# Norm tiles made in step with the output projection at two borders, and weight loads moved between state stores

## The reference, cut to what matters

```python
def rmsnorm(x, g):
    y = xf * lax.rsqrt(jnp.mean(xf * xf, axis=-1, keepdims=True) + EPS)
    return y * g
def ffn_half(x, g, wg, wu, wd):
    return x + 0.5 * swiglu(rmsnorm(x, g), wg, wu, wd)
# layer i:
xp = ffn_half(xp, *f1);  xp = xp + mixer(rmsnorm(xp, norm_mix[i]));  xp = ffn_half(xp, *f2)
```

## Time and profile before

| | us |
|---|---|
| median of 3 runs (1693.33 to 1696.01) | 1695.6 |
| the profiled execution, its time | 1693.2 |
| its span | 1691.4 |
| PE busy in it | 1655.1 (98%) |
| DVE, ACT, POOL busy | 823.6, 633.9, 283.7 |
| granted clock of PE, mean | 0.996 of full |

### The profile page before, as it was taken

One profiled execution on the slowest core, in us unless ns is written; L12 is line 12 of the kernel. 1 busy time (PEld: TensorE's weight loads), 2 busy tenths in 40 slices (PEclk: granted clock), 3 DMA queues, 4 the chain that ended last, 5 costly groups with the idle time before them and its releaser, 6 DMA issues.

```text
span 1691.4 us, 25177 instructions
## 1 busy us (share of the span) xinstructions
PE 1655.1 (98%) x9539; PEld 1581.4 (93%) x9539; DVE 823.6 (49%) x969; ACT 633.9 (37%) x765; POOL 283.7 (17%) x253
## 2 busy tenths in 40 slices
PE   7999999999999999999999999999999999999997
PEld 6999999976799999999999999898989888999997
DVE  6444444753355444445444444564646466444332
ACT  5343322354334433224344322333333344444232
POOL 2111122430031111121111022202020212111021
PEclk9999999999999999999999999999999999999999
DMA  5444344540024444345444344647475754444342
GB/s 164 124 124 128 113 120 135 164 152 32 32 75 125 126 129 123 106 128 141 129 130 128 95 125 132 239 161 257 166 253 171 251 182 124 124 124 124 103 120 89
DMA packets 341736, 231.25 MB, mean 137 GB/s; under 512 B 8429, under 2 KB 312634, under 8 KB 341690
## 3 DMA queue, kind: packets, MB, share of 16 engines
q1 hardware_dynamic: 341690, 230.61, 45.5%
HBM read 209.64 MB, written 20.94 MB: 136 GB/s over the span
## 4 chain that ended last, share of the span: by engine, by line
PE 94%; DVE 3%; ACT 1%; DMA 1%; issue 1%; SPq 0%; POOL 0%; DVEq 0%; POOLq 0%; ACTq 0%
PE bank L140 27%; PE bank L142 27%; PE bank L141 26%; PE bank L820 2%; PE bank L1332 1%; PE bank L1334 1%; PE bank L1333 1%; PE bank L841 1%; PE bank L1369 1%; PE bank L1399 1%; DMA RAW<-w_ffn_up_dram 1%; DVE WL L134 1%; PE bank L1440 1%; DVE XL L152 0%; PE bank L1358 0%
## 5 line engine op out<-in xcount | busy, mean ns | idle before, releaser
L140 PE MATMUL bank<-XH,WH 128*128 128x384 f32 x1776 | 600.1, 338 | 5.8 <-DVE XL L152 5.7
L142 PE MATMUL bank<-XH,WL 128*128 128x384 f32 x1776 | 595.3, 335 | 0.0
L141 PE MATMUL bank<-XL,WH 128*128 128x384 f32 x1776 | 595.1, 335 | 0.0
L127 ACT ACTIVATE WH<-RAW 128x2048 fp32r<-128x2048 f32 (+2 forms) x199 | 337.0, 1695 | 622.6 <-PE bank L142 578.8
L134 DVE TENSOR_TENSOR WL<-RAW,WH 128x2048 fp32r<-128x2048 f32 (+2 forms) x199 | 408.2, 2053 | 298.8 <-ACT WH L127 298.5
L140 PEld LDWEIGHTS bank<-XH,WH 128*128 128x128 f32 x1776 | 334.7, 188 | 13.8 <-issue 7.4
L141 PEld LDWEIGHTS bank<-XL,WH 128*128 128x128 f32 x1776 | 335.0, 189 | 1.1
L142 PEld LDWEIGHTS bank<-XH,WL 128*128 128x128 f32 x1776 | 334.8, 188 | 0.0
L140 PE MATMUL bank<-AH,WH 128*128 128x384 f32 x704 | 238.3, 339 | 0.0
L141 PE MATMUL bank<-AL,WH 128*128 128x384 f32 x704 | 237.8, 338 | 0.0
L142 PE MATMUL bank<-AH,WL 128*128 128x384 f32 x704 | 237.8, 338 | 0.0
(11 more groups left out here) (224 smaller groups left out, 1463.5 us busy)
## 6 DMA issues: line engine op xcount, KB each, us to landing
RAW<-w_ffn_gate_dram SPq DMA_DIRECT2D x88, 512.0 KB, 4.0
RAW<-w_ffn_up_dram SPq DMA_DIRECT2D x88, 512.0 KB, 5.2
RAW<-w_ffn_down_dram SPq DMA_DIRECT2D x64, 384.0 KB, 4.0
RAW<-w_ret_in_dram SPq DMA_DIRECT2D x48, 512.0 KB, 4.7
RAW<-w_ffn_down_dram SPq DMA_DIRECT2D x64, 320.0 KB, 3.3
st<-state_ret_dram SPq DMA_DIRECT2D x32, 512.0 KB, 7.2
new_state_sample_dram<-st SPq DMA_DIRECT2D x32, 512.0 KB, 6.2
RAW<-w_ret_out_dram SPq DMA_DIRECT2D x16, 512.0 KB, 4.2
```

Source lines behind the costliest of these rows:

```text
L127: ins = act.activation(dst(WH), src, ACT.Copy)
L140: pe.matmul(ps, wh, xh, start=first, stop=False)
L141: pe.matmul(ps, wh, xl, start=False, stop=False)
L142: return pe.matmul(ps, wl, xh, start=False, stop=last)
```

## The change

It has four parts.

1. Behind MLA the norm tiles go to tiles of their own, `X2H` and `X2L`, which the next FFN reads. ACT makes two of them behind each of its looks, DVE one behind each add into `X` (one tile late).
2. Behind retention DVE makes tile m-1 behind the add of tile m in the last head. ACT's order is as before.
3. In both FFNs that follow, PE waits at the start for the banks instead of relying on the norm tiles for it: for 7 adds behind MLA, and for the seventh add of the last head behind retention (32 counts, one of them POOL's).
4. SP loads the last FFN's chunk 0 ahead of the last head's first group of state stores, and its chunk 1 between the first and the second group.

```diff
-        def norm_tile_act(act, s, m, g, base=0):
+        def norm_tile_act(act, s, m, g, base=0, xh=XH):
...
-        def norm_tile_dve(dve, s, m, g):
+        def norm_tile_dve(dve, s, m, g, xh=XH, xl=XL):
             dve.wait_ge(sem("xh"), m + (KD * s + 1))
...
+                if self.banks_free:
+                    pe.wait_ge(sem(f"x_ready{self.s}"), self.banks_free)
                 gate_pair(0, True)
...
@@ Mla.act
-                for q in range(7, 6 + KD // 2):
-                    self.look_act(act, q)
                 act.wait_ge(sem("stored"), 16 * 2 * TT)
-                act.wait_ge(multiplied, self.c0 + self.N_CHUNKS)
-                for m in range(KD):
-                    norm_tile_act(act, self.s + 1, m, gain(KD * (self.s + 1) + m))
-                self.look_act(act, 6 + KD // 2)
+                for g in range(KD // 2):
+                    self.look_act(act, 7 + g)
+                    for m in (2 * g, 2 * g + 1):
+                        norm_tile_act(act, self.s + 1, m, gain(KD * (self.s + 1) + m), xh=X2H)
@@ Mla.dve
-                    if g < KD // 2 - 1:
-                        self.look_dve(dve, 7 + g)
-                dve.wait_ge(sem("stored"), 16 * 2 * TT)
-                for m in range(KD):
-                    norm_tile_dve(dve, self.s + 1, m, gain(KD * (self.s + 1) + m))
-                self.look_dve(dve, 6 + KD // 2)
+                        if part:
+                            self.look_dve(dve, 7 + g)
+                        if g == 0 and part == 0:
+                            dve.wait_ge(sem("stored"), 16 * 2 * TT)
+                        if m >= 1:
+                            norm_tile_dve(dve, self.s + 1, m - 1, gain(KD * (self.s + 1) + m - 1), X2H, X2L)
+                norm_tile_dve(dve, self.s + 1, KD - 1, gain(KD * (self.s + 2) - 1), X2H, X2L)
@@ Retention.sp
-                for group in range(3):
-                    store_states(RET_HEADS - 1, group)
+                self.next_ffn.load_gate(sp, 0, 0)
+                store_states(RET_HEADS - 1, 0)
+                self.next_ffn.load_gate(sp, 0, 1)
+                store_states(RET_HEADS - 1, 1)
+                store_states(RET_HEADS - 1, 2)
@@ Retention.dve
-                self.dve_head(dve, RET_HEADS - 1)
-                for m in range(KD):
-                    norm_tile_dve(dve, self.s + 1, m, gain(KD * (self.s + 1) + m))
+                self.dve_head(dve, RET_HEADS - 1, True)
+                norm_tile_dve(dve, self.s + 1, KD - 1, gain(KD * (self.s + 2) - 1))
                 self.look_dve(dve, RET_HEADS - 1, self.PER - 1)
@@ Retention.dve_head
+                    if last and m >= 1:
+                        norm_tile_dve(dve, self.s + 1, m - 1, gain(KD * (self.s + 1) + m - 1))
@@ phases
-                  Ffn(2, 1, 1, 3, c_mla + Mla.N_CHUNKS + C, whole), Retention(4, c_ret), Ffn(3, 1, 2, 5, c_last, half)]
+        last_ffn = Ffn(3, 1, 2, 5, c_last, half, banks_free=KD * RET_HEADS)
+                  Ffn(2, 1, 1, 3, c_mla + Mla.N_CHUNKS + C, whole), Retention(4, c_ret, last_ffn), last_ffn]
```

More of the change, by code:

```diff
@@ L93, in stream_kernel @@
             ytok = sb("ytok", [P, TT, D_MODEL], F32, r)
+            X2H = sb("X2H", [P, KD, T], F32R, r)
+            X2L = sb("X2L", [P, KD, T], F32R, r)
         with ExitStack() as r:
@@ L142, in product @@
             return pe.matmul(ps, wl, xh, start=False, stop=last)
-        def norm_tile_act(act, s, m, g, base=0):
+        def norm_tile_act(act, s, m, g, base=0, xh=XH):
             act.wait_ge(sem(f"x_ready{s}"), m + (base + 1))
-            act.activation(tile(XH, m), tile(X, m), ACT.Copy, scale=g).then_inc(sem("xh"), 1)
-        def norm_tile_dve(dve, s, m, g):
+            act.activation(tile(xh, m), tile(X, m), ACT.Copy, scale=g).then_inc(sem("xh"), 1)
+        def norm_tile_dve(dve, s, m, g, xh=XH, xl=XL):
             dve.wait_ge(sem("xh"), m + (KD * s + 1))
-            dve.scalar_tensor_tensor(tile(XL, m), tile(X, m), g, tile(XH, m).bitcast(F32),
+            dve.scalar_tensor_tensor(tile(xl, m), tile(X, m), g, tile(xh, m).bitcast(F32),
                                      ALU.mult, ALU.subtract).then_inc(sem("xl"), 1)
@@ L263, in stream_kernel, with __init__ @@
         class Ffn:
-            def __init__(self, f, li, which, s, c0, next_widths):
+            def __init__(self, f, li, which, s, c0, next_widths, xh=XH, xl=XL, banks_free=0):
+                self.xh, self.xl, self.banks_free = xh, xl, banks_free
                 self.f, self.s, self.c0, self.c1 = f, s, c0, c0 + KF
@@ L285, in sp @@
             def sp(self, sp):
-                first = 1 if self.c0 == 0 else 0
+                first = 1 if self.c0 == 0 or self.last else 0
                 with sp.Fori(first, KF // 2) as i:
@@ L314, in gate_pair @@
                                     pe.wait_ge(sem("xl"), KD * self.s + k + 1)
-                                mm = product(pe, ps[:, 0:T], w, k, XH[:, k, :], XL[:, k, :], k == 0, k == KD - 1)
+                                mm = product(pe, ps[:, 0:T], w, k, self.xh[:, k, :], self.xl[:, k, :], k == 0, k == KD - 1)
                             mm.then_inc(multiplied if part else self.gate_done, 1)
@@ L1194, in stream_kernel, with __init__ @@
             PARTS = 6
-            def __init__(self, s, c0):
-                self.s, self.c0 = s, c0
+            def __init__(self, s, c0, next_ffn):
+                self.s, self.c0, self.next_ffn = s, c0, next_ffn
                 self.stored = (sem("r_stored0"), sem("r_stored1"), sem("r_stored2"))
@@ L1542, in dve, with dve_head @@
                 norm_root_dve(dve, self.s + 1)
-            def dve_head(self, dve, h):
+            def dve_head(self, dve, h, last=False):
                 c = self.c0 + self.PER * h
@@ L1666, in stream_kernel @@
         whole, half = (SLOT, SLOT), (0, 0)
-        phases = [Ffn(0, 0, 1, 0, 0, whole), Mla(1, c_mla, whole), Ffn(1, 0, 2, 2, c_mla + Mla.N_CHUNKS, whole),
-                  Ffn(2, 1, 1, 3, c_mla + Mla.N_CHUNKS + C, whole), Retention(4, c_ret), Ffn(3, 1, 2, 5, c_last, half)]
+        last_ffn = Ffn(3, 1, 2, 5, c_last, half, banks_free=KD * RET_HEADS)
+        phases = [Ffn(0, 0, 1, 0, 0, whole), Mla(1, c_mla, whole), Ffn(1, 0, 2, 2, c_mla + Mla.N_CHUNKS, whole, X2H, X2L, KD - 1),
+                  Ffn(2, 1, 1, 3, c_mla + Mla.N_CHUNKS + C, whole), Retention(4, c_ret, last_ffn), last_ffn]
         block = ctx.enter_context(nc.Block())
```

## The result

The changed kernel takes 1702.9 us (median of 5 runs, 1699.87 to 1704.14), the kernel before 1695.83 (median of 5). The ratio is 1.0042, with a 95% interval of 1.0031 to 1.0053: **7.1 us slower**, outside my range (1694.0 to 1700.5), on the side that I had given a chance of 0.27. The profiled execution took 1702.9 us with a span of 1701.1, 9.7 more than the one of before.

The account below looks back on a forecast made before the run. PE was taken as the bound, busy 98% of the span, so only border waits or clock could change. Terms -0.55 + 1.2 + 2.4 = +3.05 us on the median 1695.6 gave 1698.6 us, range 1694.0 to 1700.5.

Parts of the forecast that it names:

- MLA's tiles, own operands: MLA border: tiles 0 to 5 made during the projection, while DVE and ACT sit idle, at no cost.
- rival D: MLA border: the clock falls there too, behind the new 2.4 us stand; up to 3.4 us more loss; chance 0.12.
- The MLA border, -0.55: Sum of acc 0.55 us earlier, with tiles 6 and 7 late behind chunk 1's split; bounds nothing to 3.1.
- Loads between stores: Retention border: ACT's 12.92 us wait for chunk 0 goes, PE's matmul replaces it; ACT's split ends 4.2 us earlier.
- Retention's tiles in step, +1.2: Retention border: POOL takes turns with DVE, PE waits 5.7 us for acc, the sum comes 1.2 us later.
- The clock behind that wait, +2.4: Last FFN: PE's 5.7 us wait for acc takes the clock down to 1.2 GHz, losing 2.4 us.
- rival B: Retention border: clock falls in the first stand, the wait for acc is 2.5 us; +0.65 to +1.7 us; chance 0.26.
- A: Retention border: first stand of 3.2 us leaves the clock, the second takes it down; +2 to +4.3 us; chance 0.42.
- The sum: Whole kernel: -0.55 + 1.2 + 2.4 = +3.05 us, put on the median of 1695.6.

Follow-up runs that it names:

- e1: The changed kernel with 128 bytes of padding ahead of X2H, nothing else: 1700.12 us against 1695.42 for the kernel before.
- e2: The changed kernel with the retention border's edits taken back, so only the MLA part: 1698.5 us against 1695.42 for the kernel before.
- e3: The changed kernel with the MLA border's edits taken back, so only the retention part: 1697.69 us against 1695.42 for the kernel before.
- e6: The kernel before with AH 32 and AL 256 bytes past a multiple of 512: 1689.89 us (one run) against 1694.52.
- e10: The kernel before with 384 bytes of padding ahead of all tiles: 1692.61 us (one run) against 1695.26.
- e4: The kernel before with only SP's load order at the retention border changed (chunk loads between stores): 1692.99 us against 1695.42.
- e5: The kernel before with 128 bytes of padding ahead of AH, which shifts AH and AL: 1687.06 us against 1694.52.
- e8: e3 with DVE's split of chunk 1 held back until POOL has made all of acc: 1695.43 us against 1694.52 for the kernel before.
- e9: e3 with the low norm tiles queued behind the split of chunk 0, the first after X[4]'s add: 1690.79 us against 1695.26 for the kernel before.
- e7: e2 with X2H shifted 128 bytes and norm tiles 6 and 7 ahead of chunk 1's split: 1690.66 us against 1694.52 for the kernel before.
- e11: The change with 128 bytes ahead of AH, e7's order behind MLA and e9's behind retention: 1680.65 us against 1695.26 for the kernel before.
- e12: e11 with ACT instead of POOL squaring tiles 4 to 7 behind retention: 1680.31 us against 1695.26 for the kernel before.

## Why the prediction was wrong, step by step

- **"MLA's tiles, own operands ... costs nothing": the step that failed.** I priced when the tiles are made and put what reading them costs at nothing, without looking. It is 1056 matmuls at 2.7 ns more (176.0 instead of 173.3), so 2.8 us; e1 gave 2.5 (that FFN) and 2.4 to 2.8 (median) back. With them back the kernel lies at +4.7, inside my range. The down phases of the kernel before show the price, 176 ns a matmul beside 173.3 in the gate phases, but I had taken one figure for all matmuls.
- *The clock at MLA (rival D, 0.12)*: it came, and was the second miss. Behind the stand of 2.3 to 2.4 us PE was at 1.2 GHz for 6.8 us in the change and in e1, for 3.4 in e2. Of the FFN's +5.6, 2.5 to 2.7 are the matmuls, so the clock took about 3. I had let 1.57 us kept in one execution stand for safe. Eight profiles have before's MLA border with that stand of 1.57: before, e3, e6 and e10 keep 2.4 GHz, while e4, e5, e8 and e9 have a low stretch of 3.4 us, and there the border takes 8.4 to 9.0 us instead of 7.5. e9's window (clock 0.50):

```profile
501.00:503.80 2.80, 2.80 (x10) 2.80 (x10) 2.80 (x6) 2.78 (x3) 0.00 (x0) 0.50 0.00 0
```

- *The MLA border, -0.55*: -0.22 in the profile of the change, -0.47 in e2. The mechanism (split of chunk 1 ahead of tiles 6 and 7) is shown by e7, where its removal takes the border to 4.34.
- *Loads between stores*: right. ACT's wait went, PE's matmul took its place, and e4 gives 2.8 at the border (I never priced this part alone).
- *Retention's tiles in step, +1.2*: right: +0.98, with PE's first matmul 3.2 us behind the last of the projection, as worked out, and POOL's last add done 13.0 behind it. e8 confirms the turns to 0.05 us. What I did not see is that the order, not the idea, was at fault (e9).
- *The clock behind that wait, +2.4*: +1.9 in the last FFN, +2.7 in e3's (280.55 against 277.93). The size was about right, the course was not: the clock fell at the first stand (rival B) and again at the second (A). PE's 24 matmuls were slow in between, so its wait for `acc` was 3.87 us and not 5.7.
- *The sum*: in the profiles the terms that I had priced came to -0.22 + 0.98 + 1.9 = +2.7, where I had +3.05, so that part was right in kind and size. The rest of the profile's +9.7 is the matmuls, the clock behind MLA and the chance stretch at 458. On the median 7.1 - 2.8 - 3.1 would leave +1.2, but that subtraction is rough: before's own runs may fall at MLA too, and the runs of one kernel scatter by 2 to 6 us.

## What to carry to other kernels

In these runs, making work in step with its producer paid only where nothing that others wait for stood behind it in the queue: put the first piece behind the producers' adds, and the last piece ahead of prefetch work. Where DVE and POOL both read two SBUF operands, count their instructions as turns in one line, the long splits too (POOL's add of 1.01 us took 2.95 behind one). Give an operand tile that is moved or copied the same start, modulo 512 bytes, as the tile that it replaces, and compare the matmul durations of the two.

## What the runs showed of the hardware

A matmul of 128x384 fp32r took 334 ns (173.3 between starts) or 338 (176.0). Which of the two it was went with the SBUF start of its moving operand relative to that of the weights' tiles: fast at a distance of 0 and 128 bytes modulo 512, slow at 384 and 416. In this kernel that decides 5.6 us in four down phases.

PE's clock at the MLA border: with no stand it stayed at 2.4 GHz in all three profiles (e7, e11, e12); with a stand of 1.57 us it fell in four of eight; with one of 2.3 to 2.4 us in all three (the change, e1, e2). The eight with 1.57 us run the same MLA instructions, so one profile that kept it does not show that a stand is safe. At retention, with stands of 0.8 us and less, e12's profile keeps 2.4 GHz, while those of e9 and e11 have a low stretch of 3.4 us that begins 0.7 and 1.1 us behind the start of the sum; what makes the difference is open.

DVE and POOL took whole turns where both had all inputs in SBUF: taking one split out of the line moved POOL's end, and with it the sum, by 1.80 us (e8).
